# Moving the small gates' exponentials and logarithm ahead of the shift rows in a hybrid DeltaNet / RWKV-7 / PEER step

## What is computed

```python
P    = xn @ p['w_in']                                    # projections: rwkv r, kr, vr, w/a/g; q, k, v; z; gates
beta = sigmoid(P[..., O_BETA:O_ALPHA])                   # 4 heads
g    = -exp(dn_a_log) * softplus(P[..., O_ALPHA:O_RW] + dn_dt_bias)
prw  = P[..., O_RW:O_GATE]
prev = concatenate([shift_buf, prw[:, :-1]])
mix  = prw + (prev - prw) * rw_mu                        # token shift ("mix")
shift_new = prw[:, -1:]                                  # "shift rows", an output
w_log = -softplus(-(rw_w0 + tanh(wl) @ rw_w2)) - 0.5     # wl, al, gl: last 256 columns of mix
a     = sigmoid(rw_a0 + al @ rw_a2)
gate  = sigmoid(gl) @ rw_g2
```

## Time and profile before

| | |
|---|---|
| median of 3 runs | 1151.82 us (1150.0 to 1153.03) |
| profiled execution, its own time | 1145.65 us |
| span of that execution | 1143.9 us, mean granted TensorE clock 0.984 |
| TensorE matmuls busy | 977.6 us (85%) |
| VectorE busy | 706.5 us (62%) |
| ScalarE busy | 264.4 us (23%), in it 22 table loads of 1283 ns |
| GpSimd busy | 520.9 us (46%) |
| DMA | 334.24 MB, mean 292 GB/s |

### The profile page before, as it was taken

The page is one execution under the profiler, slowest core; times in us unless marked ns, Lnnn a source line. Parts: engine busy times, 40 slices in busy tenths (PEclk is TensorE's granted clock), DMA queues, the critical chain, the costliest instruction groups (busy, mean ns, idle before and its releaser), DMA issues.

```text
span 1143.9 us, 11113 instructions
## 1 busy us (share of the span) xinstructions
PE 977.6 (85%) x3667; PEld 545.2 (48%) x3667; DVE 706.5 (62%) x1870; ACT 264.4 (23%) x635; POOL 520.9 (46%) x583
## 2 busy tenths in 40 slices
PE   6999999999999999988987777777777777777787
PEld 5876677789976448544432222222222222222221
DVE  2025864973556239884775776676686577577553
ACT  2138553022250112221131111111122111111111
POOL 2000100000000016576677677777767777777763
PEclk9999999998999998999999999999999999999999
DMA  9242022463264329999999999999999999999996
GB/s 289 85 174 80 1 77 55 133 177 75 74 220 163 111 87 404 395 378 369 409 403 406 409 409 409 405 409 409 407 393 409 408 409 410 408 409 401 396 366 261
DMA packets 121862, 334.24 MB, mean 292 GB/s; under 512 B 19119, under 2 KB 36370, under 8 KB 121542
## 3 DMA queue, kind: packets, MB, share of 16 engines
q0 software_dynamic: 76032, 276.86, 61.5%
q1 hardware_dynamic: 45642, 56.64, 15.5%
q10 hardware_dynamic: 132, 0.04, 0.0%
HBM read 326.99 MB, written 5.74 MB: 291 GB/s over the span
## 4 chain that ended last, share of the span: by engine, by line
PE 38%; DMA 29%; DVE 15%; POOL 11%; issue 5%; ACT 2%; SPq 0%; DVEq 0%; POOLq 0%
PE bank L1428 36%; DMA sb_all<-in_peer_u,idx 19%; POOL sb_all L591 11%; DMA sb_all<-in_peer_v,idx 9%; DVE sb_all L1148 5%; ACT sb_all L1869 1%; DVE sb_all L1126 1%; DVE sb_all L1124 1%; DVE sb_all L1128 1%; DMA sb_all<-in_w_in 1%; DVE key_i L1096 1%; DVE sb_all L1089 1%; ACT L1869 1%; DVE key_i L1090 1%; DVE sb_all L1093 0%
## 5 line engine op out<-in xcount | busy, mean ns | idle before, releaser
L1428 PE MATMUL bank<-sb_all 128*128 128x512 f32 (+18 forms) x3390 | 949.7, 431 | 148.4 <-DMA sb_all<-in_peer_v,idx 136.2
L1428 PEld LDWEIGHTS bank<-sb_all 128*128 128x128 f32 (+8 forms) x3390 | 518.3, 181 | 572.5 <-DMA sb_all<-in_peer_v,idx 320.1
L1148 DVE CUSTOM_DVE_ANT_0 sb_all<-sb_all,bank 128x1024 f32<-128x1024 f32 x264 | 314.8, 1220 | 186.7 <-DMA sb_all<-in_peer_u,idx 186.3
L591 POOL DMA_INDIRECT sb_all<-in_peer_u,idx x264 | 253.0, 958 | 212.6 <-issue 159.8
L591 POOL DMA_INDIRECT sb_all<-in_peer_v,idx x264 | 253.8, 961 | 88.1 <-issue 66.1
L1869 ACT ACTIVATE sb_all<-sb_all 128x128 f32<-128x128 f32 (+9 forms) x367 | 145.0, 421 | 560.9 <-PE bank L1428 369.0
L1869 ACT ACTIVATE sb_all<-bank 128x264 f32<-128x264 f32 (+18 forms) x175 | 77.3, 457 | 302.6 <-PE bank L1428 253.8
L627 POOL MEMSET sb_all<- 128x512 f32 x1 | 0.5, 525 | 136.7 <-PE bank L1428 136.7
L1418 POOL MEMSET sb_all<- 128x3456 f32 x1 | 3.0, 2987 | 127.6 <-DVE sb_all L2278 127.6
L2159 DVE SCALAR_TENSOR_TENSOR sb_all<-sb_all 128x288 f32<-128x288 f32 x14 | 6.1, 512 | 63.0 <-ACT sb_all L1869 63.0
L1869 ACT ACT_TABLE_LOAD x22 | 28.2, 1283 | 7.5 <-DVE sb_all L2299 3.9
(11 more groups left out here) (237 smaller groups left out, 402.8 us busy)
## 6 DMA issues: line engine op xcount, KB each, us to landing
sb_all<-in_w_in SPq DMA_DIRECT2D x8, 2048.0 KB, 8.8
sb_all<-in_peer_wq SPq DMA_DIRECT2D x4, 2048.0 KB, 17.4
sb_all<-in_w_in SPq DMA_DIRECT2D x6, 1024.0 KB, 5.2
sb_all<-in_peer_u,idx POOLq DMA_INDIRECT x264, 10.9
sb_all<-in_peer_v,idx POOLq DMA_INDIRECT x264, 11.0
out<-sb_all SPq DMA_DIRECT2D x8, 512.0 KB, 4.0
sb_all<-in_w_out SPq DMA_DIRECT2D x2, 2048.0 KB, 8.7
sb_all<-in_x_prompt SPq DMA_DIRECT2D x4, 512.0 KB, 4.0
```

What stands on the lines that cost most here:

```text
L591: pool.indirect_dma_start(ring[at % 8], None, table[0], bass.IndirectOffsetOnAxis(ap=idx[:, c:c + 1], axis=0)).then_inc(landed[at % 8], 16)
L1148: v.tensor_tensor_reduce(uring[i % 8], uring[i % 8], x, 1.0, 0.0, ALU.mult, ALU.add, hdot[:, u % 2, j:j + 1]).then_inc(u_free, 1)
L1428: return nc.tensor.matmul(out, lhsT, rhs, start=start, stop=stop, **kw)
```

## The change

ScalarE computes the three small-gate exponentials and the logarithm right behind the 14 mix copies and ahead of the shift rows' copies; the four q copies then stand together. VectorE forms their arguments ahead of its mixes, and waits for the two `ba` copies before it does (`ba_used`). No arithmetic is changed.

```diff
@@ ScalarE
             for f in range(14):
                 fn(mix[:, f, 0:NP], prw[:, f, 1:1 + NP], scale=omu[:, f:f + 1]).then_inc(mix_part.sem, 1)
+            act.wait_ge(ln_done, 1)
+            step(fn(gtmp, gtmp, ACT.Exp, scale=-1.0))
+            step(fn(bt, ba[:, :, 0:4], ACT.Exp, scale=-1.0))
+            step(fn(alog, alog, ACT.Exp))
+            step.sync()
+            fn(gtmp, gtmp, ACT.Ln, bias=1.0).then_inc(ln_done, 1)
             for b in range(4):
                 act.wait_ge(shift_t.sem, shift_t.at(b + 1))
...
             fn(mix[:, 13, :], mix[:, 13, :], ACT.Sigmoid).then_inc(wag_act.sem, 1)
-            evacuate([pre[:, 0, 3 + PAD:3 + NC]])
-            act.wait_ge(ln_done, 1)
-            step(fn(gtmp, gtmp, ACT.Exp, scale=-1.0))
-            step.sync()
-            step(fn(bt, ba[:, :, 0:4], ACT.Exp, scale=-1.0))
-            step(fn(alog, alog, ACT.Exp))
-            evacuate([pre[:, 1, 3 + PAD:3 + NC]])
-            step.sync()
-            fn(gtmp, gtmp, ACT.Ln, bias=1.0).then_inc(ln_done, 1)
-            evacuate([pre[:, f, 3 + PAD:3 + NC] for f in (2, 3)])
+            evacuate([pre[:, f, 3 + PAD:3 + NC] for f in range(4)])
@@ VectorE
             dve.wait_ge(consts, 2)
+            dve.wait_ge(ba_used.sem, ba_used.at(1))
+            step(tt(gt, ba[:, :, 4:8], dtb.unsqueeze(1).broadcast_to([128, 4, 4]), ALU.add))
+            step.sync()
+            step(ts(gtmp, gt, -1.0, None, ALU.mult))
+            step.sync()
+            tt(gtmp, gtmp, gt, ALU.max).then_inc(ln_done, 1)
             for f in range(14):
...
             ins.then_inc(kk0_ready, 1)
-            step(tt(gt, ba[:, :, 4:8], dtb.unsqueeze(1).broadcast_to([128, 4, 4]), ALU.add))
-            step.sync()
-            step(ts(gtmp, gt, -1.0, None, ALU.mult))
-            step.sync()
-            tt(gtmp, gtmp, gt, ALU.max).then_inc(ln_done, 1)
             dve.wait_ge(ln_done, 2)
```

## The result

| | before | after |
|---|---|---|
| median of 12 executions | 1148.66 us (1143.69 to 1153.03) | 1140.91 us (1136.66 to 1146.16) |
| ratio | | 0.995, 95% interval 0.9928 to 0.9973 |
| traced execution, its own time | 1145.65 us | 1141.43 us |
| its span, mean granted clock | 1143.9 us, 0.984 | 1139.6 us, 0.986 |
| ACT_TABLE_LOADs | 22 | 21 |

The kernel became faster, by 5.7 us after the ratio (3.1 to 8.3). The forecast was 2.8 us less, and a time of 1149.0 in a range of 1146.5 to 1152.8: the sign is right, the measured time lies outside the range.

A forecast was written before the change was run, and what follows sets the result against it. PE was taken to bound the touched stretch and the start of the gathers, which fill DMA from 430 us. Stall 1.1 plus clock 1.7 gave 2.8 us less: 1151.8 to 1149.0 us, range 1146.5 to 1152.8.

The forecast's parts named there:

- The path: PE runs without a break from 95.17 to 143.29 us, so the change is worth what it does to PE's start there.
- the slack of 1.4 us at Sigmoid's result: At PE's first lora product: Sigmoid's result, due about 90.5 us, could come 1.4 us later before PE waits.
- the load that falls away: On ScalarE, the first lora Sigmoid finds its table set loaded, so 22 loads become 21.
- VectorE's part as off the path: Earlier arguments delay the mixes by 0 to 0.6 us at no cost; earlier `g` and `beta` alone are worth nothing.
- the shift rows' delay hidden: ScalarE's shift copies come 1.8 us late, hidden by PE's two q tiles between 84.3 and 91.9 us.
- Rival C: The gain is absorbed because something that does not move decides later; time 1151.8 us, chance 0.09.
- D: Slower: PE waits at its first lora product for Sigmoid's result, delayed by ScalarE's table loads; 1154.4 us, chance 0.04.
- B: PE's idle goes but the clock falls all the same; 1.1 us less, 1150.7 us, chance 0.26.
- E: More low-clock stretches go than one, as PE's later stalls shift; a further 1.7 us, 1147.3 us, chance 0.09.
- the term "stall": PE's idle of 0.98 us before the fifth lora product goes; worth 0.98 to 1.45 us, taken as 1.1.
- a slack of 0.9 behind ScalarE's read: At the fifth lora product: ScalarE's first read ends at 93.2 us, the product starts at 94.1, 0.9 us of slack.
- The term "clock": PE's 3.4 us at half clock between 96 and 102 us goes with the idle before it; worth 1.7 us.

The follow-up runs named there:

- reload_after: Changed kernel with one unread Exp between the fourth q copy and the first lora Sigmoid, bringing two table loads; ratio 1.0021 to the kernel before.
- act_only: Kernel before with ScalarE's part of the change alone, VectorE's arguments at their old place; ratio 0.9962 to the kernel before.
- dve_only: Kernel before with VectorE's part of the change alone, ScalarE as before; ratio 1.0023 to the kernel before.
- pairs: Changed kernel with the first eight lora products in the order w0, a0, w1, a1 and so on, on both engines; ratio 0.9968 to the kernel before.
- fill_before: Kernel before with two unread matmuls (1.0 us) ahead of the fifth lora product, where TensorE stood idle; ratio 0.9985 to the kernel before.
- delay_after: Changed kernel with seven unread matmuls (3.5 us at full clock) ahead of the fifth lora product; ratio 1.0009 to the kernel before.
- before_t4: One more traced execution of the kernel before, nothing edited; 1151.98 us.

## Why the prediction was wrong in size

**The path** was right up to the start of the fifth product. The place, the slack of 1.4 us at Sigmoid's result, the load that falls away, VectorE's part as off the path, the shift rows' delay hidden, all shown by the rows above and by reload_after, act_only and dve_only. Rival C is refuted: an absorbed gain would make the rest after the stretch 4.6 us longer, and the means are both 998.7, known to 3.5 us. D did not occur; each load still took 1.28 us beside new neighbours, and the next activation began 0.01 to 0.02 us behind it, so the 1.38 us of drain in the rule of the Trainium skill's page "ScalarE: Activation LUTs" (section What ACT_TABLE_LOAD costs) does not appear here either. B did not occur in five traces. E's further stretches, in PE's later stalls, were not seen: the low-clock time there is the same (above).

**The step that failed is the fifth product's start, and with it the term "stall": 1.1 us, measured 1.9.** I had let the fifth product wait for the fourth to end, at 94.1 us, with a slack of 0.9 behind ScalarE's read. In both kernels it began 0.56 us behind the start of ScalarE's first read: at 95.17 for a read at 94.61, and at 93.40 for one at 92.84. Nothing else held it in either trace. So it gained all that ScalarE gained, 1.88 us counted from L1488 (12.41 and 10.53 us behind it), before any clock falls. At 93.40 the fourth product had not begun; TensorE ran the two side by side, as they use different row halves, and the stall had parted them. Timeline of the changed kernel in two narrow windows, up to 93.395 us and from there to 93.41, and of the kernel before at 95.1 to 95.2 (a row counts all matmuls that touch the window):

```profile
93.14 0.66 PE L1428 MATMUL bank<-sb_all 64*128 64x296 f32 x2
```

```profile
93.14 0.77 PE L1428 MATMUL bank<-sb_all 64*128 64x296 f32 x3
```

```profile
95.17 0.51 PE L1428 MATMUL bank<-sb_all 64*128 64x296 f32 x1 [0.98 <-ACT sb_all L1869]
```

The third matmul begins between the windows and ends at 93.91, 0.51 us long like the fifth product's first half in the kernel before; the two others are the third product. (The expectation of pairs took two neighbouring records 0.11 us apart for the fourth and the fifth product; the fifth began 0.24 us ahead of the fourth.) Over a longer stretch, 93.5 to 94.2 us of the changed kernel, and the kernel before from its fifth product on:

```profile
93.14 1.27 PE L1428 MATMUL bank<-sb_all 64*128 64x296 f32 x7
```

```profile
95.17 1.51 PE L1428 MATMUL bank<-sb_all 64*128 64x296 f32 x5 [0.98 <-ACT sb_all L1869]
```

Seven halves in 1.27 us against five in 1.51 (0.51 for the first and 0.25 for each more). I had read the 64 rows only as a risk for the clock, and called the term "near the matmul's row" at 1.1, inside my own bounds of 0.98 and 1.45, which the value now lies outside.

**The term "clock", 1.7 us, was one stretch of a single execution.** As such it was right (61.10 - 57.58 - 1.88 = 1.64 us). Its mean over six executions is 62.23 - 57.58 - 1.88 = 2.8 us, because in three the stretch was double and in one of these a further one followed at 120 us. I asked whether the stretch would go, with a chance, but not how long it is in other executions of the same kernel, or on another chip.

**The start and the spread were the largest part of the miss.** I carried the saving to the median of three executions, 1151.82; over twelve it is 1148.66, 3.2 us lower. And I gave an execution 1.5 us of scatter from those three, where 35 spread over 12 us. Against 1149.0 - 1140.9 = 8.1 us of miss: 3.2 are the start, 2.9 the size of the gain, and the remaining 2.0 the difference between the two medians (7.75) and the ratio (5.7). Of the 2.9, the traces place 1.8 in the two terms (4.6 for 2.8), if their mean holds for the untraced executions too; the other 1.1 lies within the intervals and has no place.

## What to carry to other kernels

A stall of one microsecond on TensorE costs what follows it too: here the stall that showed as 1.0 us of idleness cost 3.5 to 6.9 us in all, by a clock that fell to 1.2 GHz behind it for 3.4 or 6.8 us and by two products that no longer ran side by side. That the idle brings the fall is borne out at this place (8 of 8 traces with an idle of 0.98 us or more, none of 9 without one or with 0.61), but a filler in its place did not win the time back. Before moving work ahead on a helper engine, read that engine's holes (here 1.42 us) and its table loads in order; work moved into a hole ahead of a deadline with slack is free, and a set that stays loaded is a gain. And a median of three executions is no base for a forecast in tenths of a per cent where the granted clock's mean differs between executions: look at the scatter of clock and time first.

## What the runs showed of the hardware

The time of an execution goes with its mean granted clock: over twelve executions of the changed kernel from 1146.2 us at 0.982 to 1138.7 at 0.991 and 1136.7 at 0.989. TensorE's clock also fell while TensorE had been busy for over 20 us (fill_before at 117 us, delay_after and before_t4 at 120 us; what does it is open), and an idle of 0.61 us brought no fall in act_only, one of 0.98 us did in all seven traces that have it, one of 1.64 us a double one. Matmuls that use rows 0 to 63 and rows 64 to 127 in turn overlapped: eight halves of 296 columns in 1.27 us in pairs, where eight in sequence would take 2.26. By the records of the changed kernel a product on rows 64 to 127 also began ahead of one on rows 0 to 63 that stands before it in the program: the fifth at 93.40 us, the fourth at 93.64.
